# Layer order, softmax banks and folded normalisation in a two-layer decoder trunk

## The chip, the core and the metric

The kernel runs on one NeuronCore of a Trainium2 chip, as one program for the whole trunk. The metric is the device time of that program in microseconds (us), lower is better. TensorE (PE in the profile) does the matrix products, ScalarE (ACT) and VectorE (DVE) do everything element by element, GpSimd (POOL) stages keys, values and the bias of the softmax layer, SyncE (SP) issues the loads of the weights.

## The reference

Two post-norm decoder layers with 2048 features over 16 meta tokens and 256 tokens (272 in all, the meta tokens are dropped at the end), in float32. The first mixes with sliding-window softmax attention, 32 query heads of 64 on 4 key heads, with learned sinks and a bias by distance; the second with stick-breaking attention, 16 heads of 128. Each mixer's output is multiplied by a SiLU gate and projected back.

```
def branch_a(h, w_in, sinks, w_out, rel_bias):
    z = h @ w_in
    q, k, v, gate = jnp.split(z, [A_WIDTH, A_WIDTH + A_KV_WIDTH, A_WIDTH + 2 * A_KV_WIDTH], axis=-1)
    o = sliding_window_sink_attention(q, k, v, sinks, rel_bias).astype(h.dtype)
    return (o * jax.nn.silu(gate)) @ w_out
...
    for i in range(DEPTH):
        ...
        h = layer_norm(DEEPNORM_ALPHA * h + y, ln_g[i], ln_b[i])
    return h[:, N_META:]
```

Layer two's input is `(x - mu) * rstd * g + b` of the first sum, with one mean and one rstd for each token.

## The kernel before

Activations lie transposed: `h`, `x_hi`, `x_lo` hold 16 tiles (kt) of 128 features by 272 tokens. A float32 product is made of three float32r products: every operand is split into a high part (ACT, `split_hi` for weights) and a rest (DVE, `split_lo`), and `hi*hi + hi*lo + lo*hi` is summed. `project(P, ...)` (L308) makes 256 output features in two PSUM banks `acc[0]`, `acc[1]`: 16 tiles x 2 banks x 3 terms = 96 matrix products, in two halves of 48. Between the halves it calls `between()`. Each projection P takes two chunks of weights of 1 MB, (P, 0) and (P, 1). SP loads them into two raw slots, ACT writes the high part, DVE the rest, each into one of four slots that come free when the products of an earlier half have read them (`half_used`, `tile_full`). Nothing schedules at run time: each engine runs its list in the order in which it is written, and waits on counting semaphores. `lo_ready` counts the chunks that are split, `tile_full[u]` the projections summed in bank u, `tile_free[u]` the banks that have been read out; a projection P waits until `tile_free[u]` has reached P before it writes `acc[u]`.

The stages in order of time, by projection number:
- Keys and values of layer one, and queries of two iterations (P 0 to 3).
- The softmax layer, eight iterations of four heads (`body_a`). An iteration projects a gate (Pg = 2 + 2i) and the queries of the next iteration (Pg + 1), makes the scores of its four heads (`scores_of`, L440, u = 0 and 1, two heads each), and turns and multiplies the probabilities of the iteration before (`turn_a` L462 transposes through `pt_bank` = banks 4 and 5, ACT copies them out, `value_a` L481). The fourth head's scores lie in bank 2, where the first's were, so they wait for the first head to be read.
- The output projections of layer one, P_OUT_A = 18 to 25. DVE adds each result tile to `h` (`combined`, L1250) and keeps running sums of the rows (`c_sum`) and of their squares (`sq_sum`, squares by ACT).
- The normalisation (P_B = 26 follows). PE sums the rows over the partitions with `mean_w`, DVE and ACT make rstd, then for each pair of tiles n: `centre` (L1318), `scaled` (L1324), x_hi with bias (ACT L972), `rest` (L1332, x_lo) and `offset` (ACT L966, h for the residual). PE fills the wait with `spin` products (L549).
- Queries and keys of layer two's first heads together (`queries_and_keys_0` L629, P 26 and 27, banks 0, 1, 5, 6), 192 products. It takes the tiles one after the other, as they are normalised. Some chunks of weights are kept in the still unused `x_hi` and `x_lo` (`AHEAD`).
- The first iteration of layer two, `body_b(0)`: values (P 28, into banks 4 and 7), with `scores_b` between its halves; the gate (P 29, into `acc`), with `tails` and `turn_values` between its halves. The list of DVE there is: `split_lo` of the gate's two chunks, three minima on the scores (L1361, L1364), softplus and its split (L1371, L1374), the copy of the first value tile (L1381), `split_lo` of (30, 0), the copy of the second value tile (L1380, L1381). These two copies are what raises `tile_free[0]` and `tile_free[1]` to 29, for which the gate's projection waits.
- Seven more iterations of layer two, the last output projection and the last normalisation.

## Time and profile before

| | us |
|---|---|
| median of 3 runs | 904.96 |
| lowest, highest | 904.74, 905.33 |
| the profiled execution | 904.62 |
| its span, first to last instruction | 902.8 |

The profile records one execution; its times are counted from the first instruction. TensorE is busy in nearly the whole span, so the question at each place is whether anything keeps it waiting, and how many products it has to issue. The start times of two products in a row tell how long one holds the engine, since products overlap: a product of 272 columns is recorded as 0.29 us, but the next one starts about 0.126 us later.

### The profile page before, as it was taken

How to read it: one execution, taken by the hardware profiler on the slowest of the kernel's cores; microseconds unless marked ns; L12 is line 12 of the kernel's file. 1: busy time of each engine (PE TensorE's matmuls, PEld its weight loads, DVE VectorE, ACT ScalarE, POOL GpSimd, SP SyncE). 2: the span in 40 equal slices, each digit the busy share in tenths (PEclk: the TensorE clock that was granted, in tenths of full speed). 3: DMA queues.
4: the chain of work that ended last, by engine and by line, in shares of the span. 5: the costliest groups of instructions: out<-in, count | busy, mean ns of one | idle time of the engine just before them, and what ended most of it. 6: DMA issues, size and time to landing. Idle time of an engine off the chain costs nothing.

```text
span 902.8 us, 17880 instructions
## 1 busy us (share of the span) xinstructions
PE 893.6 (99%) x7182; PEld 862.2 (96%) x7182; DVE 556.0 (62%) x746; ACT 429.1 (48%) x685; POOL 62.1 (7%) x85
## 2 busy tenths in 40 slices
PE   9999999999999999999999999999999999999997
PEld 9999999999999999899999999999999999988886
DVE  6578667666765767785646464555646355545546
ACT  6556455645655344385454443535444444435421
POOL 1222033113200000000000000000000000000000
PEclk9999999999999999999999999999999999999999
DMA  9774464456442555525453534444354544454622
GB/s 344 238 237 167 154 219 139 148 166 177 155 153 105 187 187 190 184 66 212 143 187 139 181 144 163 162 145 180 139 186 139 186 144 165 156 212 162 233 94 94
DMA packets 25399, 153.05 MB, mean 170 GB/s; under 512 B 3426, under 2 KB 4210, under 8 KB 8852
## 3 DMA queue, kind: packets, MB, share of 16 engines
q1 hardware_dynamic: 21744, 142.19, 43.9%
q0 software_dynamic: 2896, 7.70, 4.2%
q10 hardware_dynamic: 724, 2.66, 0.8%
q8 instruction: 26, 0.43, 0.2%
q14 instruction: 9, 0.07, 0.0%
HBM read 150.36 MB, written 2.18 MB: 169 GB/s over the span
## 4 chain that ended last, share of the span: by engine, by line
PE 95%; DVE 2%; DMA 1%; ACT 1%; issue 0%; SPq 0%; DVEq 0%
PE bank L342 70%; PE bank L712 10%; PE bank L457 2%; PE bank L497 2%; DMA raw<-chunks 1%; PE bank L657 1%; PE bank L656 1%; PE bank L659 1%; PE bank L624 1%; PE bank L583 1%; PE bank L597 1%; PE bank L364 1%; PE bank L365 1%; PE bank L363 1%; DVE w_lo L1073 1%; PE bank L472 0%
## 5 line engine op out<-in xcount | busy, mean ns | idle before, releaser
L342 PE MATMUL bank<-x_hi,w_hi 128*128 128x272 f32 (+1 forms) x1472 | 425.6, 289 | 0.0
L342 PE MATMUL bank<-x_hi,w_lo 128*128 128x272 f32 (+1 forms) x1472 | 421.4, 286 | 0.0
L342 PE MATMUL bank<-x_lo,w_hi 128*128 128x272 f32 (+1 forms) x1472 | 421.3, 286 | 0.0
L1073 DVE TENSOR_TENSOR w_lo<-raw,w_hi 128x2048 fp32r<-128x2048 f32 x126 | 290.4, 2308 | 207.1 <-ACT w_hi L791 174.4
L791 ACT ACTIVATE w_hi<-raw 128x2048 fp32r<-128x2048 f32 x114 | 217.9, 1913 | 157.0 <-PE bank L342 104.8
L342 PEld LDWEIGHTS bank<-x_hi,w_hi 128*128 128x128 f32 x1472 | 277.4, 188 | 1.1 <-issue 0.2
L342 PEld LDWEIGHTS bank<-x_hi,w_lo 128*128 128x128 f32 x1472 | 277.4, 188 | 0.0
L342 PEld LDWEIGHTS bank<-x_lo,w_hi 128*128 128x128 f32 x1472 | 277.0, 188 | 0.0
L342 PE MATMUL bank<-og_hi,w_hi 128*128 128x272 f32 x240 | 70.1, 292 | 0.0
L342 PE MATMUL bank<-og_hi,w_lo 128*128 128x272 f32 x240 | 69.4, 289 | 0.0
L342 PE MATMUL bank<-og_lo,w_hi 128*128 128x272 f32 x240 | 69.1, 288 | 0.0
L712 PE MATMUL bank<-w_hi,og_lo 128*128 128x512 f32 (+1 forms) x144 | 53.4, 371 | 0.0
L712 PE MATMUL bank<-w_hi,og_hi 128*128 128x512 f32 (+1 forms) x144 | 53.1, 369 | 0.0
L712 PE MATMUL bank<-w_lo,og_hi 128*128 128x512 f32 (+1 forms) x144 | 52.9, 367 | 0.0
L865 ACT ACTIVATE work<-work,small 128x272 f32<-128x272 f32 (+2 forms) x96 | 38.4, 402 | 21.1 <-DVE small L1147 21.1
L342 PEld LDWEIGHTS bank<-og_hi,w_hi 128*128 128x128 f32 x240 | 45.1, 188 | 0.3
L342 PEld LDWEIGHTS bank<-og_lo,w_hi 128*128 128x128 f32 x240 | 45.2, 188 | 0.0
L342 PEld LDWEIGHTS bank<-og_hi,w_lo 128*128 128x128 f32 x240 | 45.1, 188 | 0.0
L1052 ACT ACTIVATE w_hi<-raw 128x2048 fp32r<-128x2048 f32 x12 | 23.0, 1930 | 33.8 <-DMA raw<-chunks 19.4
L712 PEld LDWEIGHTS bank<-w_hi,og_hi 128*128 128x128 f32 x144 | 27.1, 188 | 5.1
L712 PEld LDWEIGHTS bank<-w_lo,og_hi 128*128 128x128 f32 x144 | 27.1, 188 | 4.8
L712 PEld LDWEIGHTS bank<-w_hi,og_lo 128*128 128x128 f32 x144 | 27.0, 188 | 4.7
(246 smaller groups left out, 1020.0 us busy)
## 6 DMA issues: line engine op xcount, KB each, us to landing
raw<-chunks SPq DMA_DIRECT2D x128, 1024.0 KB, 4.8
work<-bias_table POOLq DMA_DIRECT2D x8, 512.0 KB, 5.6
work<-chunks SPq DMA_DIRECT2D x4, 512.0 KB, 11.5
work<-bias_table POOLq DMA_DIRECT2D x8, 256.0 KB, 6.6
work<-ln_rows ACTq DMA_DIRECT2D x1, 2048.0 KB, 7.1
out<-work SPq DMA_DIRECT2D x8, 256.0 KB, 2.4
h<-xT SPq DMA_DIRECT2D x2, 544.0 KB, 9.2
raw<-chunks SPq DMA_DIRECT2D x2, 512.0 KB, 7.3
```

Source lines behind the costliest of these rows:

```text
L342: last = mm(o, l, r, start=(kt == 0 and n == 0), stop=(kt == KT - 1 and n == 2))
L363: mm(o, whi, x_hi[:, kt, :], start=(kt == 0), stop=False)
L364: mm(o, whi, x_lo[:, kt, :], start=False, stop=False)
L365: return mm(o, wlo, x_hi[:, kt, :], start=False, stop=(kt == KT - 1))
L457: m = mm(banks[h2][0:rows, lo:lo + n], q[part, u, q_cut], k[part, 0:n], start=(step == 0), stop=(step == 2))
L497: m = mm(o[:, 0:n], l, r, start=(step == 0), stop=(step == 2))
L583: mm(z[:, 0:B_K1], k[:, 0:128], q, start=True, stop=False)
L712: last = mm(o[:, 0:cols.stop - cols.start], m[:, kt, part], w, start=(kt == 0 and n == 0), stop=(kt == KT - 1 and n == 2))
L791: A(split_views(P, half, layer_b)[0], raw[:, half, :, :], ACT.Copy).then_inc(hi_ready, 1)
L865: A(t, t, ACT.Exp, bias=neg_max[0:rows, col:col + 1], accum_out=row_sum[0:rows, col:col + 1]).then_inc(probs_exp, 1)
L1052: A(w_hi[:, B_SLOTS[c], :, :], raw[:, c % 2, :, :], ACT.Copy).then_inc(hi_ready, 1)
L1073: V.tensor_tensor(lo_part, raw[:, half, :, :], hi_part.bitcast(f32), ALU.subtract) \
```

## The change

1. Softmax layer. The fourth head's scores go to bank 4, which the transposes of the pair before have used. The order in TensorE's iteration becomes: gate, first half; values of pair 1 of two iterations ago and the turn of pair 0; gate, second half; values of pair 0; turn of pair 1; both scores; queries. ACT, DVE and GpSimd follow (`copies` of pair 1 ahead of a `split_hi`, gating of pair 1 one iteration later, keys staged ahead of values, one memset that clears part of bank 4).
2. Start. The first 256 KB of keys' and values' weights come by one transfer and are cast at once, instead of in two parts.
3. Output projections of layer one. Each tile that is summed is also split at once, times the gain g, into `x_hi` (ACT, `scaled_hi`) and `x_lo` (DVE, `scaled_rest`), not yet centred or scaled by rstd. `split_lo(P + 2, 0)` now stands ahead of `combined` everywhere.
4. Queries and keys of layer two's first heads are made from these tiles. Two more columns hold g and b (rows of x get 274 columns), so that each result tile also gets W^T g and W^T b; `unfold` on DVE and one activation on ACT then correct the result by mean and rstd. The matrix products of the statistics stand after the second tile, as two whole sums; the spin products and the broadcast of rstd are gone. The chunks of weights use the four ordinary slots (`AHEAD` is gone).
5. The tiles are normalised for the values, the gate and the residual while queries and keys are made: `normal` on ACT, `centre`, `scaled` and `rest` on DVE, each pair only after `x_used` says that its unnormalised tiles have been read. Pairs 6 and 7 stand behind the four `unfold` and one `split_lo` on DVE.

```diff
+        x_hi_all = sb("x_hi", [128, KT, T + 2], f32r)
+        x_lo_all = sb("x_lo", [128, KT, T + 2], f32r)
+        x_hi, x_lo = x_hi_all[:, :, 0:T], x_lo_all[:, :, 0:T]
...
-            return (bank[2], bank[3], bank[6], bank[2])[c]
+            return (bank[2], bank[3], bank[6], bank[4])[c]
...
-                    if m == 0:
-                        for c in range(2):
-                            sp.dma_start(kv_raw[:, 0, c, :], chunks[0][:, c * CW:(c + 1) * CW]) \
-                              .then_inc(first_loaded[c], 16)
-                        continue
...
-                    pe.wait_ge(scores_read, 2 * (4 * i + u))
+                    pe.wait_ge(scores_read, 8 * i)
+                    if u:
+                        pe.wait_ge(pt_copied, 4 * i - 1)
...
+                def values_and_turn():
+                    if not (isinstance(i, int) and i == 1):
+                        value_a(i - 2, 1)
+                    turn_a(i - 1, 0)
+
+                project(Pg, x_hi, x_lo, ALL, between=values_and_turn)
                 value_a(i - 1, 0)
-                scores_of(i, 0)
                 turn_a(i - 1, 1)
-                scores_of(i, 1)
-                project(Pg + 1, x_hi, x_lo, ALL, between=lambda: value_a(i - 1, 1))
+                for u in range(2):
+                    scores_of(i, u)
+                project(Pg + 1, x_hi, x_lo, ALL, between=(lambda: value_a(i - 1, 1)) if last else None)
...
+            def statistics():
+                pe.wait_ge(c_summed, KT)
+                mm(mean_rows, mean_w[:], ln["c_sum"], start=True, stop=True)
+                pe.wait_ge(sq_summed, KT)
+                mm(sq_rows, mean_w[:], ln["sq_sum"], start=True, stop=True).then_inc(mean_ready, 1)
...
-                            cols, banks = ((SEQ_COLS, acc), (ALL, k_acc_0))[pair]
+                            cols, banks = ((slice(META, T + 2), acc), (slice(0, T + 2), k_acc_0))[pair]
...
+                            tiles = [tiles[0], tiles[2], tiles[3], tiles[1]]
+                        pe.wait_ge(x_lo_ready, X_A + kt + 1)
+                        for n, (o, whi, wlo, xh, xl, u) in enumerate(tiles):
+                            if kt == 0 and n % 3 == 0:
                                 pe.wait_ge(tile_free[u], P_B)
-                            pe.wait_ge(pt_copied, PT_A)
-                            pe.wait_ge(x_hi_ready, X_A + 1)
-                            for o, whi, wlo, xh, _ in tiles:
-                                mm(o, whi, xh, start=True, stop=False)
-                                mm(o, wlo, xh, start=False, stop=False)
...
+                            mm(o, whi, xh, start=(kt == 0), stop=False)
+                            mm(o, whi, xl, start=False, stop=False)
+                            last = mm(o, wlo, xh, start=False, stop=(kt == KT - 1))
                             if kt == KT - 1:
-                                last.then_inc(tile_full[n % 2], 1)
+                                last.then_inc(tile_full[u], 1)
                             if kt == HALF - 1 and n % 2:
                                 last.then_inc(half_used, 1)
-                            elif kt < HALF - 1 and n == 1:
-                                last.then_inc(first_step, 1)
+                            elif kt % 2 and kt < KT - 1 and n == 3:
+                                last.then_inc(x_used, 1)
+                        if kt == 1:
+                            statistics()
...
+        FREE = {(P_B + 2, 0): (half_used, P_B + 2), (P_B + 2, 1): (half_used, P_B + 2),
+                (P_B + 3, 0): (tile_full[1], P_B + 2)}
...
+            def scaled_hi(t):
+                A(x_hi[:, t, :], h[:, t, :], ACT.Identity, scale=ln_gb[:, 0, t:t + 1]).then_inc(x_hi_ready, 1)
+
             for u in range(2):
                 square(0, u, c_ready, u + 1)
-            for n in range(6):
+                scaled_hi(u)
+            for n in range(7):
...
+            def normal(n):
+
+                step_done(act, n)
+                act.wait_ge(normed, n + 1)
+                for t in (2 * n, 2 * n + 1):
+                    gain, bias = (ln_gb[:, m, t:t + 1] for m in range(2))
+                    A(x_hi[:, t, :], h[:, t, :], ACT.Identity, bias=bias, scale=gain).then_inc(x_hi_ready, 1)
+                    act.wait_ge(x_hi_ready, X_A + KT + t + 1)
+                    A(h[:, t, :], h[:, t, :], ACT.Identity, bias=bias, scale=gain).then_inc(h_offset, 1)
+
+            for n in range(6):
+                normal(n)
+                if n in (2, 4):
+                    split_hi(P_B + 2, (n - 2) // 2)
...
+                act.wait_ge(folds_scaled, u + 1)
+                A(b["q"][:, u, :], b["w"][:, u * SEQ:(u + 1) * SEQ], ACT.Identity, bias=fold[:, u, 1:2], scale=-1.0) \
+                    .then_inc(tile_free[u], 1)
...
+            for n in (6, 7):
+                normal(n)
...
+            def scaled_rest(t):
+                dve.wait_ge(x_hi_ready, X_A + t + 1)
+                V.scalar_tensor_tensor(x_lo[:, t, :], h[:, t, :], ln_gb[:, 0, t:t + 1], x_hi[:, t, :].bitcast(f32),
+                                       ALU.mult, ALU.subtract).then_inc(x_lo_ready, 1)
+
             def out_a(P, t):
-                if P >= P_B - 3:
-                    split_lo(P + 2, 0)
-                for u in range(2):
-                    if u and P == P_B - 2:
-                        split_lo(P_B, 1)
+                split_lo(P + 2, 0)
...
-                    if u == 0 and P < P_B - 3:
-                        split_lo(P + 2, 0)
-                    if u and P == P_B - 3:
-                        split_lo(P + 2, 1)
                     dve.wait_ge(tile_free[u], P + 1)
                     V.tensor_tensor(ln["c_sum"], ln["c_sum"], h[:, t + u, :], ALU.add).then_inc(c_summed, 1)
                     dve.wait_ge(c_summed, t + u + 1)
-                    prepared(t + 2 + u)
-                if P < P_B - 3:
+                    if P < P_B - 1:
+                        prepared(t + 2 + u)
+                for u in range(2):
+                    squared(t + u, u)
+                if P < P_B - 1:
                     split_lo(P + 2, 1)
                 for u in range(2):
-                    squared(t + u, u)
+                    scaled_rest(t + u)
...
+            def unfold(n, o, width, dst, scale):
+
+
+                u = n % 2
+                dve.wait_ge(tile_full[u], P_B + 1 + n // 2)
+                V.tensor_copy(fold[:, n, 0:1], o[:, width:width + 1]).then_inc(folded, 1)
+                V.tensor_scalar(fold[:, n, 1:2], o[:, width + 1:width + 2], scale, None, ALU.mult).then_inc(folded, 1)
+                dve.wait_ge(folded, 3 * n + 2)
+                V.scalar_tensor_tensor(dst, ln["mu"][:, T - width:T], fold[:, n, 0:1], o[:, 0:width], ALU.mult,
+                                       ALU.subtract).then_inc(folded, 1)
+                dve.wait_ge(folded, 3 * n + 3)
+                V.scalar_tensor_tensor(dst, dst, scale, ln["rstd"][:, T - width:T], ALU.mult, ALU.mult) \
+                 .then_inc(folds_scaled, 1)
...
             for n in range(KT // 2):
+                if n == 6:
+                    for m in range(2):
+                        unfold(m, acc[m], SEQ, b["w"][:, m * SEQ:(m + 1) * SEQ], B_SCALE)
+                    for m in range(2):
+                        unfold(2 + m, k_acc_0[m], T, b["sp"][:, m * T:(m + 1) * T], 1.0)
+                    split_lo(P_B + 2, 1)
                 scaled(n)
                 if n + 1 < KT // 2:
                     centre(n + 1)
-                rest(n)
-                if n == KT // 2 - 3:
+                if n:
+                    rest(n - 1)
+                if n == 3:
                     split_lo(P_B + 2, 0)
+            rest(KT // 2 - 1)
```

In the output stage, DVE's list from the preparation of the third tile on, before (L1244 `prepared`, L1239 sum of squares, L1250 `combined`, L1073 `split_lo`, L1264 running sum):

```order
L1244 SCALAR_TENSOR_TENSOR h<-h,work 128x272 [waits c_summed]
L1244 SCALAR_TENSOR_TENSOR h<-h,work 128x272
L1239 TENSOR_TENSOR work<-work 128x272 [waits sq_ready]
L1239 TENSOR_TENSOR work<-work 128x272 [waits sq_ready,sq_summed]
L1250 TENSOR_TENSOR h<-h,bank 128x272 [waits prepared_rows,tile_full0,sq_summed]
L1073 TENSOR_TENSOR w_lo<-raw,w_hi 128x2048 [waits hi_ready,raw_loaded0]
L1264 TENSOR_TENSOR work<-work,h 128x272 [waits tile_free0]
```

And after (the same steps are L1231, L1226, L1237, L1055, L1249; L1241 is the new `scaled_rest`):

```order
L1231 SCALAR_TENSOR_TENSOR h<-h,work 128x272 [waits c_summed]
L1231 SCALAR_TENSOR_TENSOR h<-h,work 128x272
L1226 TENSOR_TENSOR work<-work 128x272 [waits sq_ready]
L1241 SCALAR_TENSOR_TENSOR x_lo<-h,ln_gb,x_hi 128x272 [waits x_hi_ready,sq_summed]
L1226 TENSOR_TENSOR work<-work 128x272 [waits sq_ready]
L1241 SCALAR_TENSOR_TENSOR x_lo<-h,ln_gb,x_hi 128x272 [waits x_hi_ready,sq_summed]
L1055 TENSOR_TENSOR w_lo<-raw,w_hi 128x2048 [waits hi_ready,raw_loaded0]
L1237 TENSOR_TENSOR h<-h,bank 128x272 [waits prepared_rows,tile_full0]
L1249 TENSOR_TENSOR work<-work,h 128x272 [waits tile_free0]
```

Two `scaled_rest` and the `split_lo` of the next chunk now stand ahead of the first `combined`.

TensorE's list between the last output projection and queries and keys, before (L561 sums, L549 spin, L570 broadcast of rstd, L651 and L652 first products of queries):

```order
L561 MATMUL bank<-work,mean_w 128x272
L561 MATMUL bank<-h,mean_w 128x272
L549 MATMUL bank<-parts_r,ident_r 128x256 [waits o_read,consts_ready]
L549 MATMUL bank<-parts_r,ident_r 128x256 x3
L570 MATMUL bank<-work,ident 128x136 [waits ln_step]
L570 MATMUL bank<-work,ident 128x136
L549 MATMUL bank<-parts_r,ident_r 128x256 x5
L651 MATMUL bank<-x_hi 128x256 [waits pt_copied,tile_free1,x_hi_ready,tile_free0,lo_ready]
L652 MATMUL bank<-x_hi,x_lo 128x256
L651 MATMUL bank<-x_hi 128x256
```

And after, from the second tile of keys on (L626 to L628 products of queries and keys, L596 and L598 the two sums):

```order
L626 MATMUL bank<-x_hi,w_hi 128x274
L627 MATMUL bank<-x_lo,w_hi 128x274
L628 MATMUL bank<-x_hi,w_lo 128x274
L596 MATMUL bank<-work,mean_w 128x272 [waits c_summed]
L598 MATMUL bank<-work,mean_w 128x272 [waits sq_summed]
L626 MATMUL bank<-x_hi,w_hi 128x258 [waits x_lo_ready]
L627 MATMUL bank<-x_lo,w_hi 128x258
L628 MATMUL bank<-x_hi,w_lo 128x258
```

The sums now stand inside the products, and nothing stands between the projections.

DVE's list from the last pair's rest to the first minimum, before (L1324 `scaled`, L1332 `rest`, L1073 `split_lo` of (28, 1), (29, 0), (29, 1)):

```order
L1324 SCALAR_TENSOR_TENSOR h<-h,ln_gb,bank 128x272
L1332 SCALAR_TENSOR_TENSOR x_lo<-h,ln_gb,x_hi 128x272 [waits x_hi_ready,half_used]
L1332 SCALAR_TENSOR_TENSOR x_lo<-h,ln_gb,x_hi 128x272 [waits x_hi_ready]
L1073 TENSOR_TENSOR w_lo<-raw,w_hi 128x2048 [waits hi_ready,raw_loaded1]
L1073 TENSOR_TENSOR w_lo<-raw,w_hi 128x2048 [waits hi_ready,raw_loaded0]
L1073 TENSOR_TENSOR w_lo<-raw,w_hi 128x2048 [waits hi_ready,raw_loaded1]
L1361 TENSOR_TENSOR bank<-bank,cap 128x2x128 [waits z_ready] x2
L1364 TENSOR_TENSOR bank<-bank,cap 128x32
```

And after (L1327 and L1330 the last `unfold`, L1055 the same three `split_lo`, L1309 `scaled`, L1304 `centre`, L1316 `rest`, L1362 the minima):

```order
L1327 SCALAR_TENSOR_TENSOR work<-work,small,bank 128x272 [waits folded]
L1330 SCALAR_TENSOR_TENSOR work<-work 128x272 [waits folded]
L1055 TENSOR_TENSOR w_lo<-raw,w_hi 128x2048 [waits hi_ready,raw_loaded1]
L1309 TENSOR_TENSOR h<-h,work 128x544 [waits rows_centred]
L1304 TENSOR_TENSOR h<-h,work 128x544
L1316 TENSOR_TENSOR x_lo<-h,x_hi 128x2x272 [waits h_offset,x_hi_ready,x_used]
L1309 TENSOR_TENSOR h<-h,work 128x544 [waits rows_centred]
L1316 TENSOR_TENSOR x_lo<-h,x_hi 128x2x272 [waits h_offset,x_hi_ready,x_used]
L1316 TENSOR_TENSOR x_lo<-h,x_hi 128x2x272 [waits h_offset,x_hi_ready,tile_full1]
L1055 TENSOR_TENSOR w_lo<-raw,w_hi 128x2048 [waits hi_ready,raw_loaded0]
L1055 TENSOR_TENSOR w_lo<-raw,w_hi 128x2048 [waits hi_ready,raw_loaded1]
L1362 TENSOR_TENSOR bank<-bank,cap 128x2x128 [waits z_ready] x2
```

The last two pairs' work and the `split_lo` of (28, 1) have moved behind the unfolding, ahead of the minima.

## Rows read from the trace of the kernel before

**Rows 1.** The page, part 1: busy time, share of the span and instructions of TensorE.
```profile
PE 893.6 (99%) x7182; PEld 862.2 (96%) x7182; DVE 556.0 (62%) x746; ACT 429.1 (48%) x685; POOL 62.1 (7%) x85
```

**Rows 2.** Busy time by stretch; columns: length, each engine's busy time, granted clock, DMA, GB/s.
```profile
76.35:107.09 30.74, 30.74 (x289) 29.58 (x289) 20.64 (x38) 18.59 (x42) 7.70 (x9) 1.00 0.58 188
376.10:382.20 6.10, 4.41 (x36) 3.28 (x34) 4.17 (x11) 1.75 (x5) 0.00 (x0) 1.00 0.37 153
382.18:405.78 23.60, 23.60 (x193) 23.44 (x193) 20.95 (x39) 18.00 (x36) 0.00 (x0) 1.00 0.17 54
```

**Rows 3.** TensorE in order of time, softmax layer; columns: start, duration, line, what, idle before.
```profile
75.01 0.20 PE L479 MATMUL bank<-ident,work 128*16 128x16 f32 x2
75.34 0.40 PE L457 MATMUL bank<-og_hi,parts_r 64*128 64x272 f32 x2
...
105.95 0.20 PE L479 MATMUL bank<-ident,work 128*16 128x16 f32 x2
106.08 0.39 PE L457 MATMUL bank<-og_hi,parts_r 64*128 64x272 f32 x2
```

**Rows 4.** TensorE in order of time, the first wait of the start.
```profile
7.99 0.49 PE L382 MATMUL bank<-x_hi,w_hi 128*128 128x272 f32 x2 [0.48 <-ACT w_hi L815]
```

**Rows 5.** In order of time, start of the output projections: VectorE, ScalarE, then TensorE.
```profile
300.68 0.91 DVE L1239 TENSOR_TENSOR work<-work 128x272 f32<-128x272 f32 x2
...
299.84 1.90 ACT L791 ACTIVATE w_hi<-raw 128x2048 fp32r<-128x2048 f32 x1
...
303.48 0.29 PE L342 MATMUL bank<-og_hi,w_hi 128*128 128x272 f32 x1
```

**Rows 6.** TensorE in order of time, from the last output product to the first query product.
```profile
376.00 0.29 PE L342 MATMUL bank<-og_hi,x_lo 128*128 128x272 f32 x1
...
377.72 0.72 PE L561 MATMUL bank<-work,mean_w 128*128 128x272 f32 x2
...
378.54 0.83 PE L549 MATMUL bank<-parts_r,ident_r 128*128 128x256 f32 x4
...
382.18 0.36 PE L651 MATMUL bank<-x_hi 128*128 128x256 f32 x1 [0.70 <-ACT x_hi L972]
```

**Rows 7.** In order of time, the normalisation: VectorE, then ScalarE.
```profile
379.14 0.30 DVE L1299 TENSOR_TENSOR work<-work 128x136 f32<-128x136 f32 x1 [0.80 <-ACT work L808]
379.48 0.30 DVE L1301 SCALAR_TENSOR_TENSOR work<-work 128x136 f32<-128x136 f32 x1
...
381.81 0.71 DVE L1318 TENSOR_TENSOR h<-h,bank 128x544 f32<-128x544 f32 x1
382.44 0.91 DVE L1332 SCALAR_TENSOR_TENSOR x_lo<-h,ln_gb,x_hi 128x272 fp32r<-128x272 f32 x2
...
388.72 0.92 ACT L972 ACTIVATE x_hi<-h,ln_gb 128x272 fp32r<-128x272 f32 x2
389.54 0.93 ACT L966 ACTIVATE h<-h,ln_gb 128x272 f32<-128x272 f32 x2
```

**Rows 8.** In order of time, first iteration of layer two: VectorE, then TensorE.
```profile
412.75 0.43 DVE L1361 TENSOR_TENSOR bank<-bank,cap 128x256 f32<-128x256 f32 x1
413.53 0.43 DVE L1361 TENSOR_TENSOR bank<-bank,cap 128x256 f32<-128x256 f32 x1 [0.35 <-PE bank L588]
...
418.29 0.43 DVE L1381 COPY work<-bank 128x272 f32<-128x272 f32 x1
419.64 2.29 DVE L1073 TENSOR_TENSOR w_lo<-raw,w_hi 128x2048 fp32r<-128x2048 f32 x1 [0.92 <-ACT w_hi L791]
...
421.93 0.41 DVE L1381 COPY work<-bank 128x256 f32<-128x256 f32 x1
...
419.45 0.28 PE L342 MATMUL bank<-x_hi,w_hi 128*128 128x256 f32 x1
...
422.40 0.38 PE L342 MATMUL bank<-x_hi,w_hi 128*128 128x256 f32 x1
```

**Rows 9.** Busy time by stretch, the end of the kernel; columns as in rows 2.
```profile
897.00:902.80 5.80, 1.58 (x4) 0.37 (x2) 1.41 (x3) 1.37 (x2) 0.00 (x0) 0.78 0.52 181
```

237 lines of the change are left out of this document (94 added, 143 removed).

## The prediction

> **What bounds the kernel now.** I read the page's first part, then the busy time by stretch, then the single starts of TensorE where the change touches its list, and last the lists of VectorE and ScalarE where they are behind TensorE. TensorE is busy 99% of the span [rows 1], and in the stretches that the change edits it is busy throughout at full clock [rows 2]. So an edit can win in two ways only: by issuing less between products, or by closing one of the few gaps. The big one is the normalisation: the last output product starts at 376.00 and the first query product at 382.18 [rows 6]. Elsewhere VectorE and ScalarE have spare time, and it is that time which the change spends. The sum is made on the profiled execution, 904.62 of which 902.8 is span; the median of the runs is 904.96, and I add the sum to the median.
>
> **Softmax order (saves).** No product is removed: two scores of TensorE's list change places with turns and values. What goes is four of some eight switches between long products and short ones in each of seven iterations. At one of them a value's product holds the engine from 75.01 and the scores start at 75.34, 0.33 later, while the same pair elsewhere is 0.13 apart, 105.95 to 106.08 [rows 3]: 0.20 lost, and the stretch shows no other loss, 30.74 busy of 30.74 [rows 2]. I take 0.04 for each switch removed, a fifth of that 0.20 because only one place shows it: 28 x 0.04 = 1.1. Bounds: 0.2 (that one gap alone) and 1.8. The scores of u = 1 now wait for ScalarE's copy of the turn just before them (pt_copied), which the first two heads' scores should cover; its price is a rival below. **Sum -1.1 (-1.8 to -0.2).**
>
> **Start (saves).** One transfer and one cast in place of two, one issue of SP fewer. The first wait of TensorE beside it is 0.48 [rows 4]. The bytes and the queue are the same, so I take 0.1. **-0.1 (-0.48 to 0).**
>
> **Output projections (costs).** DVE's list after the first two tiles grows. Before, it starts the two sums of squares at 300.68, 0.91 for both, and the first product into the bank freed by `combined` starts at 303.48 [rows 5]; `split_lo` comes behind `combined`. After, from 300.68: sum of squares, `scaled_rest`, again both. `scaled_rest` has the form of L1332, 0.50 each (two take 0.91 [rows 7]), so this part ends at 300.68 + 0.47 + 0.46 + 0.47 + 0.46 = 302.54. Then `split_lo` of (21, 0), whose high part ScalarE ends at 301.74 (299.84 + 1.90 [rows 5]), so it runs 302.5 to 304.7 (2.29 recorded, the next starts 0.08 earlier [rows 8]). Then `combined`, 0.44, to 305.1, and TensorE starts at 305.15. 305.15 - 303.48 = 1.67. In the later projections of the stage the same order stands, but `split_lo` comes when the 12 us of the projection's products (96 x 0.126) have mostly still to run, and the added 2 x 0.43 on each engine fits; only the start is caught. **+1.65 (1.3 to 1.9).**
>
> **The gap of the normalisation (saves).** From the last output product's end of issue, 376.13, to 382.18 are 6.05 [rows 6], and after the change queries and keys start at once, since their tiles are split during the output projections. Inside them come the two sums, 377.72 to 378.54 = 0.82 [rows 6] for four products of this kind, and two more columns: before, 193 products take 23.60 [rows 2], 0.122 each for a mean of 264 columns, so at most 0.00046 a column (0.118 for 256 columns, 0.126 for 272), x 2 x 192 = 0.18. 6.05 - 0.82 - 0.18 = 5.05, so this stage ends at 400.73 instead of 405.78. **-5.05.** Spin products and broadcast cost nothing of their own; they lay in the gap.
>
> **What takes it back: the chain on VectorE and ScalarE.** The work that the gap held (mean, rstd, centring, scaling, x_hi, x_lo, residual) is not removed. It is done beside the 24.6 us of queries and keys, on two engines that wait on one another, with more work than before. On before's clock:
> - The two sums end near 380.1 (376.13 + 24 products x 0.125 + 0.82 + the end of the last). Mean, square and variance, each 0.43 [rows 8] + 0.04 of waiting for its own result (379.14 + 0.30 to 379.48 [rows 7]): 381.5. `split_lo` of (27, 1): 383.7. Newton's three steps: 385.1. Centre and scale the first pair, 0.71 each [rows 7]: 386.6.
> - ScalarE needs 0.97 for a tile of `normal` (two activations, 0.41 and 0.51 [rows 7], the second waits for the first): 1.94 for a pair. Pairs 0 to 2 to 392.4, `split_hi` (28, 0) to 394.2 (1.90 [rows 5], the next 0.1 before its end), then VectorE's `split_lo` to 396.55; only then does VectorE scale pair 4, ScalarE works on it 397.3 to 399.25, `split_hi` (28, 1) to 401.1, pair 5 to 403.0.
> - VectorE: six steps of 0.63 to 400.36, four `unfold` of 1.14 (two of 0.43 to 0.50 that wait for each other, two tiny ones) to 404.9, `split_lo` (28, 1) to 407.1, scale pair 6 at 407.85. ScalarE pairs 6 and 7 to 411.8, `rest` of pair 7 to 412.6; the value projection then has 30 products left: 412.6 + 3.8 = 416.4, about 2 us of it waits.
> - ScalarE `split_hi` (29, 0) to 413.7, then DVE `split_lo` of (29, 0) and (29, 1), to 418.1. Only behind them stand the minima and the copy of the values. Before, the first minimum starts at 412.75 and the copy at 418.29, 5.54 later, 0.35 of it a wait for TensorE that is gone and 0.1 near it [rows 8]: 5.1, so the copy is at 423.2, not 418.29. The second copy comes 3.64 behind the first (418.29 to 421.93), its product 0.47 behind the copy (421.93 to 422.40).
> The gate's first product then starts at 423.7 instead of 419.45, its first in bank 1 at 423.2 + 3.64 + 0.47 = 427.3 instead of 422.40 [rows 8]. The latter decides: +4.9. This is the net of the last two parts, since it is a time on before's clock: the 5.05 are used up by TensorE's standing still from 416.4 to 423.7. **Net +4.9 (3.9 to 5.9)**; the bounds are one wait of 0.97 less or more in a chain of some thirty steps.
>
> The rule on which this rests: the copy cannot pass what stands ahead of it. The trace shows it: VectorE waits 0.92 for ScalarE at 419.64, and the second copy comes only behind that `split_lo`, at 421.93 [rows 8]. The Trainium skill ("TensorE: Matmul & The Clock Gate", section "Architectural detail: the array is 16× 32×32, not 1× 128×128") says the same of the two engines' queues, strictly first in, first out; without it the ready copy would pass, and the gate would start when the values end, at 416.4, as in rival (a).
>
> **Clock.** TensorE idles 7.3 us there. Before, the granted clock stays at 1.00 in the gap 376.10 to 382.20, where spin products leave only 1.69 idle [rows 2]; at the kernel's end, with 1.58 busy of 5.80, it is 0.78 [rows 9], so it falls between its two levels. If the gate starts at 1.2 instead of 2.4 GHz, its first products take twice 0.118 until it rises. Nothing in the rows says for how many: 0 to the whole first quarter of 24 products, 24 x 0.118 = 2.8 more, of which 0.8 is hidden by the wait for bank 1 (427.3 - 423.7 - 2.8). I take the middle. **+1.0 (0 to 2.0).** The Trainium skill, same page, section "What's actually happening", holds that only a part of the clock's pulses pass after TensorE was little busy, with which the two rows agree; the sum by it and without it would differ by this term, 911.3 or 910.3.
>
> **Sum.** -1.1 - 0.1 + 1.65 + 4.9 + 1.0 = +6.3. 904.96 + 6.3 = 911.3.
>
> **The rivals.**
> (a) The chain keeps pace, and the kernel is faster. If the value copy is there when the values end, the gate starts at 414.4 (400.73 + the 13.67 from 405.78 to 419.45 [rows 2, 8]): -5.05 + 1.65 - 1.2 = -4.6, 900.4; with the values' own waits of 2, 902.4, which I take for it. The point from which it decides is the first copy: at 417.8 instead of 423.2 the whole change comes to nothing, earlier it wins. For it: TensorE's list does get 5 us shorter, and two engines have idle time. Against it: from 386.6 to 418.1 VectorE has four `split_lo` (8.8), four `unfold` (4.6) and 21 steps on pairs (13.2), 26.6 of 31.5, so even without a single wait for ScalarE it would come only 4.9 earlier. Chance 0.06; 0.04 more for the part of it that ends within 0.2%.
> (b) The new wait for pt_copied bites in each of seven iterations, slower still. ScalarE's copy may be behind a `split_hi` (1.90 [rows 5]) that it has just begun; 0.5 each makes 3.5: 911.3 + 3.5 = 914.8. For it: the turn and the scores u = 1 are only the first two heads' scores apart, some 1 us. Against: ScalarE's `copies` now stand ahead of the `split_hi`. Chance 0.08.
> (c) The rows of x are 274 columns long, 1096 bytes in place of 1088. If products read such rows slower, all the products on x pay, some 4,700 of the 7182 [rows 1]: +4.7 for each ns. I bound it by 7 ns, the price of 16 columns; 1 ns gives 916.0. No row speaks for it. Chance 0.05.
> (d) The change does not do what it says in the softmax layer, the switches cost nothing: 912.2, within my own range. 0.15, with the forecast itself at 0.62.
>
> **How the numbers follow.** Forecast 0.62 and (d) 0.15 lie between 908.2 and 913.8: downward the bounds are chain 1.0, clock 1.0, order 0.7, outputs 0.35 and start 0.4, together 3.4, of which I take 3.1; upward chain 1.0, clock 1.0, order 0.9 and outputs 0.25, of which I take 2.5, since they will not all fall on one side. (a) lies below it, (b) and (c) above. Within 0.2% is 903.2 to 906.8, which is about what a measurement of this kernel tells from no change. Faster 0.07, same 0.04, slower 0.89.
>
> **What would show it.** In the profile after: no gap before queries and keys, but a wait of TensorE of some 7 us at the gate's first product of layer two, released by VectorE's copy of the values; two or so us of waits inside the values on x_lo; the first wait of the second output projection near 2 us; the softmax iterations 0.15 shorter each; a granted clock below 1.00 just after the 7 us. The forecast is wrong if that wait is under 3 us, which would mean that ScalarE's `normal` or the `unfold` are shorter than I priced them, or if the iterations grow.

## The result, and the profile after the change

The changed kernel takes 916.50 us (median of 4 runs, 916.30 to 917.27), against 904.93 in the same session: the ratio is 1.0128, with a 95% interval of 1.0116 to 1.0141. It is slower by 11.6 us, where the prediction had 6.3 and its range ended at 8.8 (913.8). The direction was right, the size was not.

The page of the changed kernel, part 1, TensorE first:

```profile
PE 895.2 (98%) x7153; PEld 864.2 (94%) x7153; DVE 562.7 (62%) x771; ACT 441.5 (48%) x702; POOL 56.1 (6%) x85
```

TensorE has 29 instructions fewer than in [rows 1] and is busy 1.6 us longer; the rest of the 11.9 us by which the span grew (914.7 against 902.8) is waiting. Its list in order of time at the places that answer to rows 3, 5, 6 and 8 (start, duration, line, what, idle before and what ended it):

```profile
74.67 0.17 PE L447 MATMUL bank<-og_hi,parts_r 64*16 64x16 f32 x2
75.44 0.39 PE L447 MATMUL bank<-og_hi,parts_r 64*128 64x272 f32 x2 [0.60 <-ACT work L852]
...
305.14 0.36 PE L330 MATMUL bank<-og_hi,w_hi 128*128 128x272 f32 x1 [1.59 <-DVE h L1237]
...
377.85 0.28 PE L626 MATMUL bank<-x_hi,w_hi 128*128 128x258 f32 x1
...
402.45 0.29 PE L330 MATMUL bank<-x_hi,w_hi 128*128 128x272 f32 x1
...
412.36 0.40 PE L330 MATMUL bank<-x_hi,w_hi 128*128 128x272 f32 x1 [0.88 <-DVE x_lo L1316]
...
427.84 0.55 PE L330 MATMUL bank<-x_hi,w_hi 128*128 128x256 f32 x1 [7.04 <-DVE work L1382]
...
435.69 0.34 PE L562 MATMUL bank<-parts_r,neg_upper_r 128*128 128x400 f32 x1
...
488.13 0.35 PE L562 MATMUL bank<-parts_r,neg_upper_r 128*128 128x400 f32 x1
```

L562 is the first product of the tails in an iteration of layer two, so its distance, 52.44, is the length of an iteration. The same two products in the kernel before, 52.21 apart:

```profile
425.30 0.34 PE L597 MATMUL bank<-parts_r,neg_upper_r 128*128 128x400 f32 x1
...
477.51 0.35 PE L597 MATMUL bank<-parts_r,neg_upper_r 128*128 128x400 f32 x1
```

From such rows the span's 11.9 us come apart by stages:

| stretch | before | after | difference | forecast |
|---|---|---|---|---|
| start, keys and values, softmax | 275.13 | 275.03 | -0.1 | -1.2 |
| output projections of layer one | 101.00 | 102.82 | +1.8 | +1.65 |
| gap, queries and keys | 29.65 | 24.60 | -5.05 | -5.05 |
| first values to first product of the gate | 13.67 | 25.39 | +11.7 | +9.3 |
| gate's first half, to the tails | 5.85 | 7.85 | +2.0 | +1.6 |
| seven iterations, to the last projection | 374.87 | 376.47 | +1.6 | 0 |
| last projection and last normalisation | 102.6 | 102.5 | -0.1 | 0 |

The stretches end with the first output product (275.13), the first product of queries (376.13 as the issue of the last output product; 377.85), the first of values (405.78; 402.45), the first of the gate (419.45; 427.84) and the tails (425.30; 435.69). The forecasts of the fourth and fifth row are the prediction's 423.7 and its 0.6 for the second copy with 1.0 for the clock. So the wait of 7 us at the gate, released by VectorE's copy (L1382), is there as described, the gap is closed as described, and three things are missing: the softmax layer gained nothing, the chain to the copy was 2.4 longer, and layer two's loop, where TensorE's list is the same, is slower throughout. The first row is the least certain: in the seven traces that share the changed kernel's list up to there, the first output product starts at 275.03 to 275.85, and the changed kernel's own is the earliest. The waits for x_lo inside the values are 3.2 in all (0.88, 1.07 and 1.29) instead of the 2 forecast; they cost nothing of their own here, since the copy comes later still.

Where the chain lengthened is seen on ScalarE. Its groups by line and shape in the changed kernel (columns: count, busy us, mean ns, idle before):

```profile
L944 ACT ACTIVATE h<-h,ln_gb 128x272 f32<-128x272 f32 x16 | 9.8, 615 | 0.5
L942 ACT ACTIVATE x_hi<-h,ln_gb 128x272 fp32r<-128x272 f32 x16 | 9.7, 604 | 7.2 <-DVE h L1309 7.2
L922 ACT ACTIVATE x_hi<-h,ln_gb 128x272 fp32r<-128x272 f32 x16 | 8.1, 508 | 0.0
```

L922 has one value per partition (the gain) and takes 0.51, as L972 and L966 of before did with the bias alone (two take 0.92, 0.41 apart [rows 7]). L942 and L944, the two of `normal`, have both, gain and bias, and take 0.61. I had priced them with 0.51.

### The profile page after: what moved, and what is told of

The parts are those of the page before. It is cut to its first block, busy times and chain, and to the rows that moved or that the text cites. A ratio compares the mean times of both kernels' runs of the same rounds, so it can differ in the third digit from the quotient of the medians.

```text
span 914.7 us, 17882 instructions
## 1 busy us (share of the span) xinstructions
PE 895.2 (98%) x7153; PEld 864.2 (94%) x7153; DVE 562.7 (62%) x771; ACT 441.5 (48%) x702; POOL 56.1 (6%) x85
## 4 chain that ended last, share of the span: by engine, by line
PE 91%; DVE 4%; ACT 2%; issue 1%; DMA 1%; DVEq 0%; ACTq 0%; SPq 0%
PE bank L330 67%; PE bank L684 10%; DVE w_lo L1055 2%; PE bank L489 2%; PE bank L447 1%; DMA raw<-chunks 1%; PE bank L589 1%; PE bank L562 1%; PE bank L548 1%; ACT x_hi L942 1%; ACT w_hi L764 1%; PE bank L351 1%; PE bank L353 1%; PE bank L352 1%; PE bank L464 1%
## 5 line engine op out<-in xcount | busy, mean ns | idle before, releaser
L1055 DVE TENSOR_TENSOR w_lo<-raw,w_hi 128x2048 fp32r<-128x2048 f32 x128 | 295.6, 2313 | 214.6 <-ACT w_hi L764 182.1
L764 ACT ACTIVATE w_hi<-raw 128x2048 fp32r<-128x2048 f32 x116 | 221.4, 1911 | 159.9 <-PE bank L330 117.6
L330 PE MATMUL bank<-og_hi,w_hi 128*128 128x272 f32 x256 | 74.4, 291 | 1.6 <-DVE h L1237 1.6
L330 PE MATMUL bank<-og_lo,w_hi 128*128 128x272 f32 x256 | 74.2, 290 | 0.0
L330 PE MATMUL bank<-og_hi,w_lo 128*128 128x272 f32 x256 | 73.9, 288 | 0.0
L330 PEld LDWEIGHTS bank<-og_hi,w_hi 128*128 128x128 f32 x256 | 48.2, 188 | 2.0 <-DVE w_lo L1055 1.8
L330 PEld LDWEIGHTS bank<-og_hi,w_lo 128*128 128x128 f32 x256 | 48.2, 188 | 0.0
L330 PEld LDWEIGHTS bank<-og_lo,w_hi 128*128 128x128 f32 x256 | 48.1, 188 | 0.0
L1034 ACT ACTIVATE w_hi<-raw 128x2048 fp32r<-128x2048 f32 x12 | 22.9, 1928 | 33.8 <-DMA raw<-chunks 19.3
## 6 DMA issues: line engine op xcount, KB each, us to landing
work<-chunks SPq DMA_DIRECT2D x4, 512.0 KB, 11.6
```

What stands on the lines that cost most here:

```text
L330: last = mm(o, l, r, start=(kt == 0 and n == 0), stop=(kt == KT - 1 and n == 2))
L764: A(split_views(P, half, layer_b)[0], raw[:, half, :, :], ACT.Copy).then_inc(hi_ready, 1)
L1034: A(w_hi[:, B_SLOTS[c], :, :], raw[:, c % 2, :, :], ACT.Copy).then_inc(hi_ready, 1)
L1055: V.tensor_tensor(lo_part, raw[:, half, :, :], hi_part.bitcast(f32), ALU.subtract) \
```

## The experiments

A kernel whose name begins with b_ is the kernel before with one edit, with a_ the changed kernel with one or more. Every ratio is to the kernel before, timed on the same chip in turns.

**Is it the row length?** `b_rows274` changes nothing but the allocation, and with it the views of the chunks kept ahead in `x_hi` and `x_lo`:

```diff
-        x_hi = sb("x_hi", [128, KT, T], f32r)
-        x_lo = sb("x_lo", [128, KT, T], f32r)
+        x_hi_all = sb("x_hi", [128, KT, 274], f32r)
+        x_lo_all = sb("x_lo", [128, KT, 274], f32r)
+        x_hi, x_lo = x_hi_all[:, :, 0:T], x_lo_all[:, :, 0:T]
...
```

> The kernel before with one edit: the tiles of x_hi and x_lo have rows of 274 elements instead of 272 (two unused columns). Nothing else. In the trace of the changed kernel an iteration of layer two's loop takes 52.44 us instead of 52.22, though its list of TensorE is the same, and its products of 256 columns start 119.3 ns apart instead of 118.5. Theory P (row length): the products that stream x tiles are slower when the rows are 1096 bytes apart. Then this kernel is slower than before by 7 x 0.22 = 1.5 in layer two and by 0.3 to 1.1 in layer one, 1.8 to 2.6 us in all, and its loop takes 52.44. Rival Q (slots or queues): the 0.22 come from the new order of the weights' slots or of VectorE's list. Then this kernel stays at 904.9 and its loop at 52.22.

Measured: 907.41, ratio 1.0027 (1.0016 to 1.0039), 2.3 us more, from two unused columns. The tails of the first two iterations of its layer two:

```profile
426.88 0.34 PE L598 MATMUL bank<-parts_r,neg_upper_r 128*128 128x400 f32 x1
...
479.31 0.35 PE L598 MATMUL bank<-parts_r,neg_upper_r 128*128 128x400 f32 x1
```

52.43, the changed kernel's length. Theory P holds, Q falls: 0.22 for 384 products on x in an iteration, 0.6 ns each.

`a_rows288b` gives the changed kernel rows of 288 elements. These alone need 1792 bytes more of each partition, more than there is room for (`a_rows288`, which so has no time). The rest of the edit makes room: `work` is shorter, and the shift row of the last normalisation lies in `h`.

```diff
-WORK = 2 * 2 * D
+WORK = 7680
...
-        x_hi_all = sb("x_hi", [128, KT, T + 2], f32r)
-        x_lo_all = sb("x_lo", [128, KT, T + 2], f32r)
+        x_hi_all = sb("x_hi", [128, KT, 288], f32r)
+        x_lo_all = sb("x_lo", [128, KT, 288], f32r)
...
-        f = carve([("r", (2, D)), ("gb", (2, D))])
+        f = carve([("r", (2, D)), ("g", (1, D))])
         h_flat = h.rearrange("p a b -> p (a b)")
+        f["b"] = h_flat[:, 2176:2176 + D].rearrange("p (a b) -> p a b", b=D)
...
```

> The changed kernel with rows of x of 288 elements (1152 bytes, a multiple of 64 as 1088 was) instead of 274. To make room, the shift row of the last normalisation moves from work into h, where it is loaded after h has been turned, and work is 7680 long instead of 8192; nothing waits for that row. b_rows274 has shown that 274 costs 2.3 us in the kernel before, with a loop of 52.44. Theory P1 (what counts is the alignment of a row's start): the loop of layer two goes back to 52.22 and the softmax iteration from 30.70 to 30.60, 2.1 to 2.4 less than the changed kernel: 914.2. Theory P2 (any distance other than the row's own length costs): 916.5, with a loop of 52.44.

Measured: 912.42, ratio 1.0083 (1.0069 to 1.0096), 4.1 less than the changed kernel, nearly twice what P1 said. Its tails:

```profile
434.39 0.34 PE L563 MATMUL bank<-parts_r,neg_upper_r 128*128 128x400 f32 x1
...
486.36 0.34 PE L563 MATMUL bank<-parts_r,neg_upper_r 128*128 128x400 f32 x1
```

51.97: not back at 52.21 but below it. So rows of 1088 bytes were not the best either, which `b_rows288` tests in the kernel before.

> The kernel before with rows of x of 288 elements instead of 272 (and the shift row of the last normalisation kept in h, to make room); nothing else. In a_rows288b the products of 256 columns on x came 117.6 ns apart and the loop took 51.97, against 118.5 and 52.22 in the kernel before and 119.3 and 52.44 with rows of 274. Theory P3 (the distance of the rows sets the product's time, and 1152 bytes is better than 1088 too): loop 51.97, 7 x 0.25 = 1.75 less in layer two, 0.5 less in layer one, 902.7. Rival: the 51.97 come from the changed kernel's other slots for the weights, not from the rows: 904.9, loop 52.22.

Measured: 903.50, ratio 0.9981 (0.9972 to 0.9990), 1.7 less, and the tails again 51.97 apart, in another kernel with other slots:

```profile
426.05 0.34 PE L599 MATMUL bank<-parts_r,neg_upper_r 128*128 128x400 f32 x1
...
478.02 0.34 PE L599 MATMUL bank<-parts_r,neg_upper_r 128*128 128x400 f32 x1
```

P3 holds, and the two prices in the kernel before, 2.3 and 1.7, add up to the 4.1 of `a_rows288b`. Averaged over some 1,400 starts of products of 256 columns on x that follow one another without a pause, the distance is 118.1 ns with rows of 272 elements, 119.1 with 274 and 117.2 with 288 (the 118.5, 119.3 and 117.6 of the expectations hold some pauses); of 272 columns it is 126.0, 126.4 and 125.8. Rows of 288 are not better for every width: queries and keys of layer two's first heads, with 258 and 274 columns, take 24.79 in `a_rows288b` against 24.60 in the changed kernel. What it is about the distance (a multiple of 64 or 128 bytes, or where the rows lie, since other buffers moved too) three values cannot tell. P2 falls, since rows of 288 are faster than 272; P1 had the direction, but not the size.

**Does the softmax order save anything?** `b_softmax` is the kernel before with part 1 of the change alone, as its diff has it.

> The kernel before with the new order of the softmax layer alone (fourth scores in bank 4, both scores behind both turns, values of pair 1 in the next gate, staging of GpSimd), rows of 272. The prediction gave this part -1.1 us. In the trace of the changed kernel a softmax iteration takes 30.70 instead of 30.73, and there is one new wait of 0.60 in the first iteration. If the row length ate the gain (theory P): -0.13 for each of 7 iterations and +0.6 once, that is -0.3, with iterations of 30.60. If the switches between long and short products cost nothing: +0.4, with iterations of 30.70 or more.

Measured: 904.35, ratio 0.9994 (0.9985 to 1.0003), -0.8 of 905.12 and not told from nothing. In its trace the same turn comes round every 30.62 us, against 30.73 before and 30.70 in the changed kernel (five iterations each), so an iteration does gain 0.11. From the first score-table product to the first output product it takes 243.94 against 244.39, 0.45 less: 7 x 0.11, less a new wait of 0.35 in the first iteration:

```profile
75.64 0.39 PE L459 MATMUL bank<-og_hi,parts_r 64*128 64x272 f32 x2 [0.35 <-ACT work L887]
```

The gain is there, though the median does not show it for sure. In the changed kernel the rows of 274 take most of it back: its iteration is 0.03 shorter than before instead of 0.11, as they also lengthen the iteration of the kernel before, from 30.73 to 30.81 in `b_rows274`. 7 x 0.03 = 0.2 is less than the new wait, 0.60 here and 0.55 to 0.81 in the six other kernels with rows of 274 and this list, so that the same stretch takes 244.76, 0.4 more than before. The table's -0.1 holds 0.5 of an earlier start of the stretch (30.27 instead of 30.74), which those six, at 30.39 to 30.98, do not repeat in the main; nothing here shows what the single transfer is worth.

**Is ScalarE's `normal` what made the chain longer?** `a_bias_only`:

```diff
-                    gain, bias = (ln_gb[:, m, t:t + 1] for m in range(2))
-                    A(x_hi[:, t, :], h[:, t, :], ACT.Identity, bias=bias, scale=gain).then_inc(x_hi_ready, 1)
+                    act.wait_ge(normed, t + 1)
+                    bias = ln_gb[:, 1, t:t + 1]
+                    A(x_hi[:, t, :], h[:, t, :], ACT.Identity, bias=bias).then_inc(x_hi_ready, 1)
...
-                V.tensor_tensor(hh, hh, on_pair(ln["rstd"]), ALU.mult).then_inc(normed, 1)
+                for t in (2 * n, 2 * n + 1):
+                    V.scalar_tensor_tensor(h[:, t, :], h[:, t, :], ln_gb[:, 0, t:t + 1], ln["rstd"],
+                                           ALU.mult, ALU.mult).then_inc(normed, 1)
```

The second activation of `normal` loses its gain in the same way.

> The changed kernel with the gain moved from ScalarE's normal to VectorE's scaled, in the kernel before's form (two steps of 272 columns with gain and rstd); ScalarE adds the bias alone. In the trace of the changed kernel an activation with gain and bias per partition takes 0.61, against 0.51 priced, so a pair takes 2.33 instead of 1.94. Theory N (the mis-sized activation is on the chain): an activation here takes 0.51, a pair 1.94, and as the pairs 0 to 2, 4 and 5, and 6 and 7 stand on the chain, the first value copy comes 1.0 to 2.0 earlier (VectorE pays 0.2 more for each pair, some of it on the chain): 914.5 to 915.5. Rival: VectorE is the bound there and its 8 x 0.2 eat the gain: 916.5 or more.

Measured: 914.73, ratio 1.0100 (1.0083 to 1.0117), 1.8 less than the changed kernel. The two lines of `normal` there, and the gate:

```profile
L944 ACT ACTIVATE h<-h,ln_gb 128x272 f32<-128x272 f32 x16 | 8.4, 524 | 0.5
L942 ACT ACTIVATE x_hi<-h,ln_gb 128x272 fp32r<-128x272 f32 x16 | 8.2, 512 | 6.9 <-DVE h L1309 6.9
```

```profile
426.49 0.55 PE L330 MATMUL bank<-x_hi,w_hi 128*128 128x256 f32 x1 [7.05 <-DVE work L1383]
```

With one value per partition the activation is back at 0.51, and the gate starts at 426.49, counted from the first output product (275.60 there, 275.03 in the changed kernel) 1.9 earlier, although VectorE has 0.2 more for each pair. Theory N holds; the wait itself is as long as before, because the values end earlier by the same amount.

**The order in the output projections.** `a_out_order`:

```diff
-                split_lo(P + 2, 0)
+                if P > P_OUT_A + 1:
+                    split_lo(P + 2, 0)
                 for u in range(2):
                     combined(P, u, t + u)
+                    if P == P_OUT_A + 1 and u == 0:
+                        split_lo(P + 2, 0)
```

> The changed kernel with split_lo of (21, 0) behind the first combined of the output projections, as it stood in the kernel before; nothing else. The prediction put the wait of TensorE that its new place makes at 1.65, the trace of the changed kernel has the product at 305.14 instead of 303.48, with 1.59 of idle time in front. Theory: with scaled_rest still ahead of it combined comes at 302.6 instead of 304.8 and the product at 303.0 to 303.5, so -1.6: 914.9. Rival: the wait moves to the next chunk, since split_lo of (21, 0) ends 0.4 later: -1.2 or less.

Measured: 914.96, ratio 1.0104 (1.0087 to 1.0121), 1.5 less. No wait is left there: at 303.55 to 304.93 its products follow each other every 0.13. The theory holds.

**What does the clock cost?** Busy time by stretch around the gate in the changed kernel (length, each engine's busy time, granted clock, DMA, GB/s):

```profile
420.00:424.00 4.00, 0.80 (x7) 0.57 (x5) 3.02 (x5) 1.31 (x4) 0.00 (x0) 1.00 0.64 238
424.00:428.00 4.00, 0.16 (x1) 0.20 (x2) 2.59 (x5) 3.74 (x7) 0.00 (x0) 0.70 0.69 287
428.00:432.00 4.00, 4.00 (x19) 4.00 (x20) 3.40 (x4) 2.30 (x2) 0.00 (x0) 0.50 0.00 0
432.00:436.00 4.00, 4.00 (x33) 4.00 (x32) 1.51 (x1) 0.05 (x1) 0.00 (x0) 0.94 0.95 336
```

It falls to 0.50 within the wait and is back at 432.4; 21 products are 0.213 apart instead of 0.119. Two kernels fill the wait with products that nobody reads, 56 in `a_filled` and 40 in `a_filled40`:

```diff
+                if isinstance(i, int):
+                    for _ in range(40):
+                        mm(bank[6][:, 0:256], ident_r[:], x_hi[:, 0, 0:256], start=True, stop=True)
                 project(P + 3, x_hi, x_lo, SEQ_COLS, between=mid, layer_b=True)
```

> The changed kernel with 56 idle products of 256 columns (ident_r on x_hi, into bank 6, read by nobody) on TensorE between the values and the gate of layer two's first iteration, 56 x 0.118 = 6.6 us in the wait of 7.04. Theory C (the clock that fell costs time of its own): the gate starts as before at 427.8, its first 21 products are at 0.119 instead of 0.213, the first bank's part ends 2.0 earlier, the second starts by its copy (430.89) at 431.4 instead of 432.8, so 1.4 to 2.0 us less than the changed kernel: 914.5 to 915.1. Rival: the clock's price is hidden by the wait for the second bank's copy and by later slack: 916.5.

Measured with 56 of them: 916.20, ratio 1.0125 (1.0108 to 1.0142). Inconclusive: in its trace the clock had already fallen in the values, between whose products the waits for x_lo leave TensorE idle, and the 56 products overran the copy (it starts at 427.36, the gate at 429.39):

```profile
416.00:420.00 4.00, 3.43 (x16) 3.14 (x15) 2.88 (x2) 3.55 (x2) 0.00 (x0) 0.50 0.00 0
```

> a_filled with 40 idle products instead of 56 (4.7 us in the wait of 7.04). In a_filled the clock fell already in the values (0.50 from 416 to 420), so that they ended 1.4 late, and the 56 products ran past the copy and held the gate up until 429.4: that run did not tell the clock's price. With 40 they end before the copy even if the values are 1.4 late. Theory C (the clock at 0.50 after the wait costs the gate 21 products at 0.213 instead of 0.119, of which 0.5 is hidden by the second copy): 914.8 to 915.2. Rival (the clock falls anyway, in the waits for x_lo or at the copy): 916.2 to 916.5.

Measured with 40: 915.76, ratio 1.0117 (1.0101 to 1.0132). Its gate starts in the same place, 152.81 after the first output product as in the changed kernel, and at full clock:

```profile
428.00:432.00 4.00, 3.17 (x25) 3.00 (x25) 3.09 (x5) 2.88 (x2) 0.00 (x0) 1.00 0.00 0
```

```profile
428.41 0.36 PE L330 MATMUL bank<-x_hi,w_hi 128*128 128x256 f32 x1 [0.71 <-DVE work L1385]
...
434.92 0.53 PE L562 MATMUL bank<-parts_r,neg_upper_r 128*128 128x400 f32 x2
```

From the gate's first product to the tails it takes 6.51 (428.41 to 434.92) instead of 7.85: in this pair of traces the clock costs 1.3. The spans differ by 0.7 only, because this trace is 0.6 later at its first output product, a stage that the edit does not touch. The medians too differ by 0.7, between what theory C (1.3 to 1.7) and its rival (0 to 0.3) expected, and their intervals overlap; as the clock also fell in the values of this run (0.68 from 416 to 420), the rival, that part of it is paid anyway, is not excluded.

**Is it the order or the amount of work?** `a_copies_first` moves the two value copies on VectorE behind `split_lo` of (29, 1), ahead of the minima (`values_out` is the loop with the copies, L1377 to L1383 of the changed kernel, made a function):

```diff
                 split_lo(P + 3, 1, True)
+                if isinstance(i, int):
+                    values_out()
                 for u in range(2):
                     dve.wait_ge(z_ready, 2 * i + u + 1)
```

> The changed kernel, with VectorE's two copies of the first value tiles moved to stand right behind split_lo of (29, 1), ahead of the minima and the softplus. In the changed kernel TensorE ends the values at 420.7 and waits 7.04 us for the copy at 427.25; split_lo of (29, 1) ends at 422.2. Theory F (the list's order, not the amount of work, makes this wait): the gate starts at 422.8, the wait is 2 us, 5.0 us are saved, and the clock does not fall, which saves another 1.5 to 2.0 for the gate's first 21 products, now at 0.213 instead of 0.119: 916.5 - 6.8 = 909.7. If softplus is then late for the gate's middle, 0 to 1 us of it is lost. Rival W (the two engines' total work sets the end): the wait moves to the tails in the gate's middle, and less than 2 us are saved: above 914.5.

Measured: 916.18, ratio 1.0118 (1.0103 to 1.0134): nothing won. TensorE and the ScalarE instruction that explains it:

```profile
423.58 0.36 PE L330 MATMUL bank<-x_hi,w_hi 128*128 128x256 f32 x1 [0.67 <-DVE work L1366]
...
442.22 0.77 PE L589 MATMUL bank<-work 128*128 128x256 f32 x1 [4.76 <-ACT work L1008]
```

```profile
438.70 1.91 ACT L764 ACTIVATE w_hi<-raw 128x2048 fp32r<-128x2048 f32 x1 [6.79 <-DMA raw<-chunks]
```

The wait at the gate falls from 7.04 to 0.67. The gate starts 147.73 after the first output product instead of 152.81, 5.1 earlier, as theory F said; the rest of the 6.4 is no gain, since the values end 1.3 later, the clock having fallen in them (0.50 from 417.04 to 420.45). 19 us later a new wait of 4.76 stands before the product with the weights of attention: ScalarE's exponentials are queued behind a `split_hi` that waits 6.79 for its load, which could start only when `split_lo` of (30, 0) had emptied the raw slot (issued at 432.68, landed at 438.67). The first iteration's tails come 60.22 before the second's instead of 52.44: 7.8 lost, with the fallen clock (0.53 from 444 to 448). This is the trace of the slowest of four executions (917.91; the fastest took 914.95), so the 7.8 are the price in that one. `a_loop_order` also moves (30, 0) to where the loop has it, on both engines:

```diff
-                if not isinstance(i, int):
-                    split_hi(P + 4, 0, True)
+                split_hi(P + 4, 0, True)
...
-                if isinstance(i, int):
-                    split_hi(P + 4, 0, True)
...
-                if not isinstance(i, int):
-                    split_lo(P + 4, 0, True)
+                split_lo(P + 4, 0, True)
...
```

> As a_copies_first, and in layer two's first iteration the split of chunk (30, 0) stands where the loop has it: ScalarE's split_hi ahead of the softplus, VectorE's split_lo right behind the minima. In a_copies_first TensorE waited 4.76 us at 442.22 for ScalarE's exponentials of the tails, which stood behind split_hi of (31, 0), which waited 6.79 us for its load, which could start only when split_lo of (30, 0) was done at 432.5, and the clock fell again (the iteration took 60.22 instead of 52.44, so 7.8 lost). Theory F (list order): split_lo of (30, 0) is done by 427, the load is there by 433.5, the wait of 4.76 and the fall of the clock go; 6 to 7.8 us less than a_copies_first: 908.4 to 910.2. Rival W (total work): most of it comes back at another wait: above 913.

Measured: 913.99, ratio 1.0096 (1.0079 to 1.0112), 2.5 less than the changed kernel and outside what F expected:

```profile
423.39 0.35 PE L330 MATMUL bank<-x_hi,w_hi 128*128 128x256 f32 x1 [1.95 <-DVE work L1363]
431.68 0.45 PE L562 MATMUL bank<-parts_r,neg_upper_r 128*128 128x400 f32 x1 [2.31 <-DVE parts_r L1383]
```

The wait moved again, to the tails, and the first iteration still takes 54.08 instead of 52.44. Again a load is behind it. ScalarE's `split_hi` of (30, 0), now ahead of the softplus, waits for it:

```profile
425.65 1.92 ACT L764 ACTIVATE w_hi<-raw 128x2048 fp32r<-128x2048 f32 x1 [5.54 <-DMA raw<-chunks]
```

It was issued at 420.87, when `split_lo` of (29, 0) had emptied the slot, and landed at 425.62. The result lies in the range that W named, above 913, and up to here W explains as much as F: each repair shows the next wait. `a_combined` puts all priced edits together.

> The changed kernel with the four edits that the runs so far have priced one by one: rows of x of 288 (2.2 by b_rows274), split_lo of (21, 0) behind the first combined (1.5 by a_out_order), gain by VectorE and bias alone by ScalarE (1.8 by a_bias_only), value copies first and chunk (30, 0) in the loop's order (2.5 by a_loop_order). If the four prices add up: 916.5 - 8.0 = 908.5. Theory W (VectorE and ScalarE together still bound the first iteration of layer two): TensorE goes on waiting some 2 us for x_lo in the values, 2 for the value copy and 2.5 for the tails. If rows of 288 do not help: 910.7.

Measured: 905.73, ratio 1.0011 (1.0002 to 1.0021). The four prices add up to more than their sum, 10.8 instead of 8.0, of which 1.9 is that rows of 288 are worth 4.1 and not 2.2, and 0.9 is not assigned. Ten executions spread over 904.67 to 907.97; in the one traced (905.35) the granted clock is 0.50 from 420.15 to 423.57, inside the gate's first half. Still, 1.95 at the gate and 0.89 at the tails are left:

```profile
418.73 0.35 PE L331 MATMUL bank<-x_hi,w_hi 128*128 128x256 f32 x1 [1.95 <-DVE work L1369]
...
427.04 0.46 PE L563 MATMUL bank<-parts_r,neg_upper_r 128*128 128x400 f32 x1 [0.89 <-DVE parts_r L1389]
```

`a_reordered` keeps every operation of `a_combined` and changes the lists of VectorE and ScalarE between 382 and 436. It also makes one move in TensorE's list: the first scores of layer two stand behind the values instead of between their halves. What that move is worth by itself was not tested. Its steps, c centre, s scaled, r rest, n normal (pair), l and h the split of chunk 0 = (28, 0), 1 = (28, 1), 2 = (29, 0) and so on, u unfold, q and k the copies of queries and keys, v value copies:

```
VectorE  c0 s0 c1 c2 c3 c4 s1 c5 s2 s3 s4 r0 l0 c6 r1 c7 r2 s5 l1 r3 u0 s6 r4 r5 s7 u1 r6 r7 u2 u3 l2
         minima v0 v1 l3 softplus, its rest, l4 l5 gates l6 heads l7
ScalarE  n0 n1 h0 n2 h1 n3 n4 n5 n6 n7 h2 q0 q1 k0 k1 h3
         softplus, its high part, h4 h5 tails gates h6 heads h7
```

> As a_combined, with the same operations of VectorE and ScalarE between the last output projection and the second iteration of layer two in another order, and the first scores of layer two behind the values instead of between their halves. Both engines take pairs 5 to 7 before the unfolding, ScalarE takes split_hi of (28, 0) and (28, 1) between the first pairs, and the split of (29, 1) stands behind the value copies. Theory F (the order in the two lists makes the waits, the work as such has room beside TensorE): worked out row by row with the durations of the two traces, one wait of 1.1 is left before the gate and none at x_lo or the tails, so the 5 us of the closed gap stay won: 904.9 - 4.1 = 900.8, range 900 to 903. Theory W (total work is the bound): no faster than a_combined by more than 2 us.

Measured: 898.12 (897.66 to 898.93), ratio 0.9923 (0.9909 to 0.9936), better than the 900 to 903 that was expected. The only wait of TensorE between the outputs and the loop, the tails after it, and the page's part 1:

```profile
415.48 0.36 PE L331 MATMUL bank<-x_hi,w_hi 128*128 128x256 f32 x1 [1.05 <-DVE work L1404]
...
421.15 0.34 PE L563 MATMUL bank<-parts_r,neg_upper_r 128*128 128x400 f32 x1
```

```profile
PE 889.2 (99%) x7153; PEld 858.4 (96%) x7153; DVE 562.6 (63%) x779; ACT 439.2 (49%) x702; POOL 55.8 (6%) x85
```

VectorE has the work it had in the changed kernel (562.6 and 562.7), and 7.6 us are gone against `a_combined`. W falls: the amount fits beside TensorE, the order made the waits. The 7.6 hold the clock too, which stays at 1.00 through this stretch in the trace of `a_reordered`; what the waits and what the clock cost is not told apart. Of the 7.0 us by which it is ahead of the kernel before, 1.7 are what `b_rows288` measured for the rows and 0.8 what `b_softmax` has for the order; that leaves 4.5 for the closed gap. The traces give it directly: from the last output product to the tails it takes 45.35 (375.80 to 421.15) instead of 49.30 (376.00 to 425.30), 3.95 less.

## Why the prediction was wrong in size

- **The gap, 5.05, and the output projections, 1.65:** right, both to 0.2 (-5.05 and +1.8; `a_out_order` gives 1.5 back). Their working from rows 5 and 6 holds. That the gap comes out to the last digit is luck: the two sums took 0.72 (380.79 to 381.51) instead of 0.82, and the longer rows, put at nothing, lengthen queries and keys from 23.60 to 23.78 in `b_rows274`.
- **The chain on VectorE and ScalarE:** right as a mechanism, in the order and at the distances forecast up to the first pair (ScalarE takes it up at 388.42; the forecast's 386.6 is 388.3 on the changed kernel's clock, where queries start 1.72 later), then too short, mostly by one term. The step that failed is "ScalarE needs 0.97 for a tile of `normal`": 0.51 was read from an activation with the bias alone (L966), and the changed one has gain and bias, 0.61. A pair takes 2.33 instead of 1.94; pairs 0 to 2 and 6 and 7 stand on the chain, 5 x 0.39 = 2.0 of the 2.4 by which the gate was later; 0.4 are spread over the chain. `a_bias_only` gave 1.8 back. By itself this error would have left the time at 913.7, just inside the range; with the row length it lies outside. The bound of one wait of 0.97 did not cover an activation that was mis-sized thirty-two times. The Trainium skill ("ScalarE: Activation LUTs", section "What ACT_TABLE_LOAD costs") has the term that I left out: each per-partition operand of an activation adds some 93 ns. This case agrees, with 512 to 604 ns for the same line.
- **Row length, rival (c):** named, given 0.05, and wrongly made a matter of 1 ns or nothing ("1 ns gives 916.0"). It is 0.4 to 1.0 ns a product, 2.3 us in `b_rows274`, of which 1.5 in layer two's loop (7 x 0.22) and the rest ahead of it. This is the second step that failed: a term put at nothing because "no row speaks for it". It belonged in the range with its small values. The Trainium skill ("SBUF — State Buffer", section "Door 1: The DMA port swizzle (why `[64,N]` ≈ `[32,N]`)") says that SBUF has lines of 16 bytes and that going over to a new one costs. 1096 is no multiple of 16, as 1088 and 1152 are, which agrees with the loss in `b_rows274`; it does not explain that 1152 is faster than 1088.
- **Softmax order, -1.1:** the size per iteration was near (0.11 for a forecast of 0.16), but the new wait for ScalarE's copy (rival (b)) bites, once and not seven times, for 0.35 in `b_softmax`, 0.60 in the changed kernel and up to 0.81 in those with the same list. By `b_softmax` the part is -0.8 with an interval that reaches 0.
- **Rival (a), that the chain keeps pace:** not so in the changed kernel. But the argument against it, that VectorE's work would bring the copy only 4.9 earlier even without a wait, took the list's order as given. With the order of `a_reordered` the gate starts 14.76 after the first value product, instead of 25.39 here and 13.67 before.
- **Clock, +1.0 (0 to 2.0):** 1.3 in a pair of traces, within the bounds.
- **The rule of the queues,** that the copy cannot pass what stands ahead of it, stood: in `a_copies_first` the order alone brought the gate 5.1 earlier. What the prediction did not see is that the same rule, through a load behind a raw slot, kept the next waits ready behind the first.

The errors of the table had one sign: chain 2.4, loop 1.6, first stage 1.1, gate's first half and output projections 0.5 to 0.6, together 5.6. My range took its bounds as if they would partly cancel.

## What to carry to other kernels

When work is taken out of a gap and laid beside TensorE, the gain can be decided by the order of the lists, and not by the helper engines' busy share: the same operations took 905.7 in one order and 898.1 in another, with two lists rearranged and one group of products moved on TensorE. After each repair look for the wait that stood behind the one removed, a load that waits for its slot among them. A new operation is priced from a row with the same operands, each per-partition value included, and a change of a buffer's row length is a change of every product that streams it.

## What the runs showed of the hardware

- Rows of the streamed tiles 1088, 1096 and 1152 bytes apart give products of 256 columns every 118.1, 119.1 and 117.2 ns, in at least two kernels each; products of 272 columns change less (126.0, 126.4, 125.8). In whole: +2.3 us for 1096 and -1.7 for 1152 against 1088.
- An activation over 272 columns takes 0.51 with one value per partition, be it gain or bias, and 0.61 with both.
- In the changed kernel the granted clock fell to 0.50 within the wait of 7.04 us, and the first 4.6 us of products after it ran so, 21 of them at 0.213 instead of 0.119. In the traces of `a_rows288b`, `a_filled`, `a_filled40` and `a_copies_first` it had already fallen in the values, where waits of 0.9 to 1.3 us for x_lo stand between groups of six products. In `a_reordered`, with a single wait of 1.05, it did not fall there.
- A load of a chunk of 1 MB landed 5 to 6 us after its issue in the two cases above (432.68 to 438.67, 420.87 to 425.62), which is what an engine queued behind it waits for.
